# The gated DeltaNet rounds of a decoder kernel: the convolution's last tap from ScalarE, the two chunk inversions as one, and the state readout later in the round

## The chip, the cores and the metric

The kernel runs on one core of a Trainium2 chip. Its time is the device time of one execution in microseconds; the median of three is given. The core's engines run side by side and meet at semaphores: TensorE (PE in the profile) multiplies, VectorE (DVE), ScalarE (ACT) and GpSimd (POOL) work element by element, SyncE (SP) issues the weight transfers.

## The reference

One inference step of a trunk with two layers, for 256 prompt tokens in two chunks of 128 and for 8 sequences of 4 sampled tokens (288 columns in all). Layer 0 has the gated DeltaNet mixer, layer 1 a Mamba-2 mixer. Only the first is touched:

```python
proj = hn @ w_in                                  # q, k, v, z, a, b
qkv, new_buf = causal_conv(qkv, conv_buf, conv_w) # 4 taps, depthwise
qkv = silu(qkv)
q, k = l2norm(q) * 128**-0.5, l2norm(k)
beta, g = sigmoid(b), -exp(A_log) * softplus(a + dt_bias)
a_mat = (k*beta) @ k.T * decay * strict           # per chunk and head
t_mat = inverse(eye + a_mat)
u, w = t_mat @ (v*beta), t_mat @ (k*beta*exp(g))
# scan over chunks: v_new = u - w S;  o = (q*exp(g)) S + (q k.T * decay) v_new
# S = S*exp(g_last) + k_dec.T v_new.  Sampled tokens: the same rule on their own states
o = rmsnorm(o) * silu(z);  out = o @ w_out
```

All is float32. A product with weights is formed from three fp32r products: high x high, low x high, high x low part.

## The kernel before

**Projection.** Weights come as tiles of 2048 x 128 in two halves of 512 KB. SyncE loads a half into `ring`, ScalarE copies it to the high part `wh` (`upper`, L787; a tile's two halves are `ahead`), GpSimd subtracts to get the low part `wl` (`lower`, L324, four instructions for a half), and TensorE multiplies (`project`, L347 to L349) into one of two PSUM banks `psj`. A bank is reused when its consumer has counted up `took_act`.

**The DeltaNet rounds.** After six tiles ahead of the loop, a loop of 15 rounds and a last one outside it handle one pair of value heads each. In round m TensorE runs 48 *slots*, e = 0 to 47, of six projection matmuls for round m+1; that is six tiles: q and k (tiles T_GLOOP and +1), z of round m (+2, +3), v (+4, +5). Behind each slot `gdn_mix(m, e)` may insert matmuls of round m's attention. So the order on TensorE is written out by hand by slot number, and a wait in an insertion stops the projection too.

**What round m inserts.** e = 0: products of the chunks' keys and queries (counts `g_tok`). e = 3: transposes of `gMK` (L402, waits for `g_mk`), and 16 matmuls that read the sampled sequences' states, the *readout* (L407, waits for the state transfer `g_st_in`). e = 5: transposes of `gDE` (waits for `g_e1`). e = 7 to 19: the inversion of `eye + a_mat` in six levels, for each of the two chunks c apart: `inv_p(c, lv)` multiplies, VectorE masks (`mask_p`, L1448), `inv_q(c, lv)` multiplies, VectorE subtracts (`less_q`, L1459 and L1461). The chunks alternate, so that one has the array while the other is on VectorE. e = 10 waits for `g_bs`, an operation on VectorE (L1474) that stands behind tap 1 of v's convolution. e = 19: transposes of v. e = 21 to 31: values, states, outputs; e = 27 waits for `vnds` from ScalarE (L1000). e = 36: transposes of the normalized output (waits for `g_on`). e = 39: the column sums for the norms of the next q and k (L354).

**ScalarE in a round**, in this order: decay matrices (`g_dte`: six Relu, one Exp, L926 to L932), copies, take tiles q and k from `psj` (L855, L856), Silu of v, copies of values, z, Silu and squares of q and k, roots, take of tile +4, the transfers of the next round's rows, v parameters and states (`g_load`), take of tile +5. After a take comes `ahead`.

**VectorE in a round**: waits for the rows, copies the round's columns, forms `gMK` and `gMQ` (L1411), then the decayed products (L1417 to L1426, ending with `g_e1`), the sampled part (to L1434, `g_as`), then the six levels with the four taps of v's convolution among the first four (L1366 is tap 0, L1368 taps 1 to 3), and so on to the next q and k: taps, norms (`g_kn`).

Of the kernel before, what the change touches and what calls it, by code (L numbers as in the profile page):

```python
# [22 lines left out]
P = 128  # L23
D_MODEL = 2048
KT = D_MODEL // P
SEQ = 256
# [53 lines left out]
SMP_PE = {n: i + 1 for i, n in enumerate(("kmt", "smp", "ast", "sqs", "esp", "us", "osm"))}  # L80
SMP_ACT = {n: i + 1 for i, n in enumerate(("kmc", "asc", "qs", "vnds"))}
G_DVE_LINKS, S_DVE_LINKS = 19, 27
# [23 lines left out]
def packed(ap, lv):  # L106

    return ap.rearrange("p (j i s) -> p j i s", j=2, s=2 << lv)
# [25 lines left out]
def build(nc, weights, x_in, p_in, prm_in, cst_in, gpack, spack, gstate, sstate,  # L134
          y_out, gconv_out, sconv_out, gst_p, gst_s, sst_p, sst_s,
          g_rows, s_rows, h_spill, G_DVE, G_ACT, S_DVE, S_ACT):
    with ExitStack() as ctx:
# [24 lines left out]
        def carve(sizes):  # L162
            out, at = {}, 0
            for name, n in sizes:
# [13 lines left out]
                    ("pc", PC_G), ("co", 4 * CW), ("cc", 16), ("sc", 5 * GV), ("scc", 10), ("MS", 2 * NS),  # L178
# [16 lines left out]
        gcc = ga["cc"].rearrange("p (k c j) -> p k c j", k=4, c=NC)  # L195
        gscc = ga["scc"].rearrange("p (k j) -> p k j", k=5)
# [9 lines left out]
        gDE = ga["DE"].rearrange("p (c k j t) -> p c k j t", c=NC, k=2, j=2)  # L206
# [129 lines left out]
        def _(pe):  # L336
# [42 lines left out]
            def gdn_ready(m, e):  # L379
# [3 lines left out]
                if e == 10:  # L383
                    pe.wait_ge(S("g_bs"), m + 1)
                if e == 27:
                    pe.wait_ge(S("g_sample_act"), m * 4 + SMP_ACT["vnds"])

            def gdn_mix(m, e, more):
# [10 lines left out]
                if e == 3:  # L399
                    pe.wait_ge(S("g_mk"), m + 1)  # L400
                    for r in range(2):
                        mm = pe.transpose(psF[:, r * P:(r + 1) * P], gMK[:, 4 * r:4 * r + 4, :], ident)  # L402
                    mm.then_inc(S("g_sample_pe"), 1)
                    pe.wait_ge(S("g_st_in"), m * 16 + 16)
# [5 lines left out]
                if e == 5:  # L410
                    pe.wait_ge(S("g_e1"), m + 1)
                    for c in range(NC):
                        for j in range(2):
                            mm = pe.transpose(psB[:, (2 * c + j) * P:(2 * c + j + 1) * P], gDE[:, c, 1, j, :], ident)
# [6 lines left out]
                def inv_p(c, lv):  # L421
# [4 lines left out]
                    else:  # L426
                        pe.wait_ge(S(f"g_de{c}"), m * 6 + lv)
                    for j in range(2):
# [1506 lines left out]
```

## Time and profile before

| quantity | value |
|---|---|
| median of three runs | 2826.65 us (2825.04 to 2834.03) |
| the profiled execution | 2822.21 us, its span 2820.4 us |
| TensorE matmul busy | 2514.7 us, 89% |
| VectorE, ScalarE, GpSimd busy | 1486.1, 1170.1, 1666.4 us |
| mean granted TensorE clock | 0.950 of full speed |

The rounds of the DeltaNet layer lie between about 74 and 1340 us. The timeline view gives one row for a run of like instructions of one line: start, duration, engine, line, operation, output and input; in brackets how long the engine had been idle before it and what it waited for. A duration includes the pipeline's depth, so successive starts tell what an instruction occupies. "PEclk" is the granted clock of a stretch as a share of full speed (1.0 is 2.4 GHz, 0.5 is 1.2 GHz).

### The profile page before, as it was taken

To read this page: it belongs to the slowest core of one execution; us is meant where nothing else is said; L and a number is where in the kernel's file an instruction comes from. 1 tells how busy PE (TensorE), PEld (TensorE's weight loads), DVE (VectorE), ACT (ScalarE), POOL (GpSimd) and SP (SyncE) were. 2 spreads that over 40 slices of the span, in tenths; PEclk is the share of its full clock that TensorE was granted. 3 is DMA by queue.
4 is the path that set the end of the run, shared out by engine and by line. 5 is a ranking of instruction groups with operands and counts; after the bars stand their busy time and mean duration, and the time that the engine had idled before them with its cause. 6 is when DMAs were issued, how large, how long until landed. Compare 5 with 4: busy or idle time off the path is not lost.

```text
span 2820.4 us, 57876 instructions
## 1 busy us (share of the span) xinstructions
PE 2514.7 (89%) x20918; PEld 2295.1 (81%) x20918; DVE 1486.1 (53%) x3373; ACT 1170.1 (41%) x2073; POOL 1666.4 (59%) x2236
## 2 busy tenths in 40 slices
PE   6988898988988889898999988888898889799997
PEld 5877777877877778787999888877887779699987
DVE  5555555555556555555132426676767776722242
ACT  4433343433343344434333444444454435433343
POOL 4544444434444454434887667666766677598765
PEclk8999999999999999999999999999999999899999
DMA  4333333323333333322644336545654466354433
GB/s 183 115 128 120 135 120 135 107 105 109 129 120 128 127 135 120 127 95 103 215 154 153 115 124 237 180 134 174 228 189 147 162 214 201 108 213 150 153 119 116
DMA packets 126773, 410.86 MB, mean 146 GB/s; under 512 B 21344, under 2 KB 37984, under 8 KB 122112
## 3 DMA queue, kind: packets, MB, share of 16 engines
q1 hardware_dynamic: 81216, 295.75, 30.0%
q10 hardware_dynamic: 45504, 114.38, 11.7%
q8 instruction: 37, 0.61, 0.1%
q14 instruction: 16, 0.13, 0.0%
HBM read 363.47 MB, written 46.61 MB: 145 GB/s over the span
## 4 chain that ended last, share of the span: by engine, by line
issue 34%; POOL 31%; PE 22%; DVE 10%; ACT 2%; DMA 1%; POOLq 0%; ACTq 0%; DVEq 0%
POOL wl L324 31%; PE psj L347 6%; PE psj L349 6%; PE psj L348 6%; DVE arena L1368 5%; DVE arena L1366 2%; ACT arena L1205 1%; DVE arena L1706 1%; DVE arena L1697 1%; PE psA L736 1%; PE psE L354 1%; DVE arena L1704 1%; PE psE L691 0%; PE psA L354 0%; DMA arena<-s_rows_d 0%
## 5 line engine op out<-in xcount | busy, mean ns | idle before, releaser
L324 POOL TENSOR_TENSOR wl<-ring,wh 128x256 fp32r<-128x256 f32 x2232 | 1666.2, 785 | 1131.4 <-ACT wh L787 1130.3
L347 PE MATMUL psj<-xh,wh 128*128 128x288 f32 x4400 | 1390.5, 316 | 105.3 <-DVE arena L1474 59.6
L348 PE MATMUL psj<-xl,wh 128*128 128x288 f32 x4400 | 1316.2, 299 | 0.0
L349 PE MATMUL psj<-xh,wl 128*128 128x288 f32 x4400 | 1311.4, 298 | 0.0
L347 PEld LDWEIGHTS psj<-xh,wh 128*128 128x128 f32 x4400 | 841.4, 191 | 182.1 <-issue 80.9
L348 PEld LDWEIGHTS psj<-xl,wh 128*128 128x128 f32 x4400 | 845.2, 192 | 6.5 <-issue 3.9
L349 PEld LDWEIGHTS psj<-xh,wl 128*128 128x128 f32 x4400 | 845.3, 192 | 0.0
L787 ACT ACTIVATE wh<-ring 128x1024 fp32r<-128x1024 f32 x558 | 564.9, 1056 | 245.1 <-PE psj L349 217.3
L1368 DVE SCALAR_TENSOR_TENSOR arena<-arena 128x256 f32<-128x256 f32 (+1 forms) x672 | 287.9, 494 | 2.6
L855 ACT ACTIVATE arena<-psj 128x256 f32<-128x256 f32 x112 | 43.1, 385 | 472.6 <-PE psj L349 462.0
L407 PE MATMUL psD<-h 128*32 128x256 f32 x512 | 75.1, 460 | 32.8 <-DMA h<-gstate_d 32.8
L1621 DVE TENSOR_TENSOR arena<-Y,arena 128x288 f32<-128x288 f32 x32 | 14.7, 458 | 163.2 <-ACT arena L1076 162.5
L1597 DVE TENSOR_TENSOR h<-h,psj 128x288 f32 x32 | 14.5, 454 | 162.1 <-PE psj L349 162.1
L1366 DVE TENSOR_SCALAR arena<-arena 128x256 f32<-128x256 f32 x224 | 93.5, 486 | 0.0
L678 PE MATMUL psA<-cst,arena 128*128 128x128 f32 x16 | 7.2, 448 | 94.5 <-ACT arena L1205 94.5
L407 PEld LDWEIGHTS psD<-h 128*32 128x32 f32 x512 | 34.1, 130 | 70.0 <-DMA h<-gstate_d 36.7
L678 PEld LDWEIGHTS psA<-cst,arena 128*128 128x128 f32 x16 | 3.3, 206 | 96.4 <-ACT arena L1205 96.4
L1587 DVE COPY Y<-psj 128x288 f32 x22 | 10.1, 457 | 131.6 <-PE psj L349 131.6
L1459 DVE TENSOR_TENSOR arena<-arena,psF 128x128 f32<-128x128 f32 x80 | 23.1, 289 | 91.2 <-PE psF L359 91.2
L1076 ACT ACTIVATE arena<-psj 128x288 f32<-128x288 f32 x32 | 13.1, 410 | 130.5 <-PE psj L349 130.5
L1448 DVE TENSOR_TENSOR arena<-psC,cst 128x128 f32<-128x128 f32 x96 | 27.1, 282 | 70.7 <-PE psC L359 70.7
L359 PE MATMUL psA<-arena 128*64 128x64 f32 x1408 | 64.0, 236 | 0.0
(311 smaller groups left out, 2999.2 us busy)
## 6 DMA issues: line engine op xcount, KB each, us to landing
ring<-weights_d SPq DMA_DIRECT2D x558, 512.0 KB, 3.3
h<-gstate_d ACTq DMA_DIRECT2D x16, 1024.0 KB, 8.7
gst_s_d<-h ACTq DMA_DIRECT2D x16, 1024.0 KB, 3.9
h<-sstate_d ACTq DMA_DIRECT2D x32, 512.0 KB, 6.3
sst_s_d<-h ACTq DMA_DIRECT2D x32, 512.0 KB, 5.0
arena<-g_rows_d ACTq DMA_DIRECT2D x16, 864.0 KB, 4.6
arena<-s_rows_d ACTq DMA_DIRECT2D x8, 1152.0 KB, 7.6
h_spill_d<-h ACTq DMA_DIRECT2D x2, 2304.0 KB, 7.8
```

Source lines behind the costliest of these rows:

```text
L324: ins = pool.tensor_tensor(wl[:, s, n:n + 2], ring[:, s, n:n + 2], wh[:, s, n:n + 2].bitcast(F32), ALU.subtract)
L347: pe.matmul(out, w_h, xh[:, kt, :], start=(kt == 0), stop=False)
L348: pe.matmul(out, w_h, xl[:, kt, :], start=False, stop=False)
L349: mm = pe.matmul(out, w_l, xh[:, kt, :], start=False, stop=(kt == KT - 1))
L354: return pe.matmul(out, ones, rhs, start=start, stop=stop)
L359: mm = pe.matmul(bank[r:r + 64, cols], lhsT[:, r:r + 64], rhs, start=True, stop=True)
L407: mm = pe.matmul(psD[NS * n:NS * n + NS, 0:2 * P], (gMK, gMQ)[n][:, b, :], gS[:, b, :, :], start=(b == 0), stop=(b == DEC_B - 1))
L736: pe.matmul((psA, psB, psC, psF)[g][:, :], sBM[rows, r, :], sXT[rows, :], start=True, stop=True).then_inc(S("s_sp"), 1)
L787: act.activation(wh[:, hc % 4], ring[:, hc % 4], ACT.Copy).then_inc(wh_ready, 1)
L855: return lambda bank: (act.activation(U[:, i, UP:UC], bank[:, 0:SEQ], ACT.Copy), act.activation(U[:, i, US:UW], bank[:, SEQ:T], ACT.Copy))[1]
L1366: ins = dve.tensor_scalar(out, src, tap(i, j), None, ALU.mult)
L1368: ins = dve.scalar_tensor_tensor(out, src, tap(i, j), out, ALU.mult, ALU.add)
```

## The change

Five things are done together, all in the DeltaNet layer.

1. **Last tap.** When ScalarE takes a q, k or v tile, it first writes `gCR` = tile x tap 3 with one more Copy with a scale (`g_take_u`). VectorE adds three taps in place of four, and its tap 0 accumulates (`begun=True`).
2. **One inversion.** The two chunks are inverted together: `inv_p(lv)` at e = 7 + 2 lv, `inv_q(lv)` at e = 8 + 2 lv, each with both chunks' matmuls. VectorE's instructions span both chunks (128 x 256). `inv_q` counts `g_qd` after its first half and `g_qe` after its second.
3. **Readout.** `gMK`'s transposes and the readout go from e = 3 to e = 18, now into `psD`; `gMK` and `gMQ` are formed after `g_as`.
4. **Decays.** The decay matrices of round m+1 are formed at the end of round m, between the takes of tiles +4 and +5 (`g_decays`); the round's columns are copied by VectorE behind `states(0)`. Beta is multiplied in ahead of the wait for `g_tok`. The rows are loaded early in round m, once `g_rf` is counted; `EG` keeps the columns that are needed later.
5. **Slots.** The wait for `g_bs` goes from e = 10 to e = 12; v's transposes from 19 to 17; the insertions of 21 to 31 each one slot earlier; output transposes from 36 to 37; the column sums from 39 to 40.

```diff
-                if e == 10:
+                if e == 12:
                     pe.wait_ge(S("g_bs"), m + 1)
-                if e == 27:
+                if e == 26:
                     pe.wait_ge(S("g_sample_act"), m * 4 + SMP_ACT["vnds"])
...
+                def inv_p(lv):
+                    if lv == 0:
+                        pe.wait_ge(S("g_d"), m + 1)
+                        pe.wait_ge(S("g_sample_act"), m * 4 + SMP_ACT["asc"])
+                    else:
+                        pe.wait_ge(S("g_dd"), m * 5 + lv)
+                    for u in range(4):
+                        mm = halves(psC, slice(u * 64, (u + 1) * 64), gAT[:, u, :], half(gDE[:, 0], lv, 0)[:, u])
+                    mm.then_inc(S("g_p"), 1)
+                def inv_q(lv):
+                    pe.wait_ge(S("g_pm"), m * 6 + lv + 1)
+                    if lv < 5:
+                        for u in range(4):
+                            mm = halves(psA, slice(u * 64, (u + 1) * 64), gDE[:, 1, u, :], half(gP[:, :], lv, 0)[:, u])
+                        mm.then_inc(S("g_qd"), 1)
+                    for u in range(4):
+                        mm = halves(psE, slice(u * 64, (u + 1) * 64), gP[:, u, :], half(gDE[:, 1], lv, 1)[:, u])
+                    mm.then_inc(S("g_qe"), 1)
...
-                if e == 39 and more:
+                if e == 40 and more:
                     pe.wait_ge(S("g_su"), m * 4 + 2)
                     gdn_norm(m + 1)
...
+            def g_take_u(i, m, bank):
+                act.wait_ge(S(("g_pq_in", "g_pv_in")[i // 2]), m * 16 + 16)
+                act.activation(gCR[:, i, :], bank[:, 0:T], ACT.Copy, scale=gpc_tap[i // 2][:, i % 2, CONV_W - 1:CONV_W])
+                take_u(i, gU)(bank).then_inc(took_act, 1)
...
                 if full:
                     tile_wait(m, per, T_GLOOP + 4)
-                    take_u(2, gU)(psj[T_GLOOP % 2]).then_inc(took_act, 1)
+                    g_take_u(2, m + 1, psj[T_GLOOP % 2])
                     ahead(m, per, T_GLOOP + 6)
+                if full:
+                    g_decays(m + 1)
...
+                def less_q(lv):
                     if lv < 5:
+                        dve.wait_ge(S("g_qd"), m * 5 + lv + 1)
+                        D = half(gDE[:, 0], lv, 0)
+                        dve.tensor_tensor(D, D, packed(psA[:, 0:2 * P], lv), ALU.subtract).then_inc(S("g_dd"), 1)
+                    dve.wait_ge(S("g_qe"), m * 6 + lv + 1)
+                    E = half(gDE[:, 1], lv, 1)
+                    dve.scalar_tensor_tensor(E, packed(psE[:, 0:2 * P], lv), cst[:, K_BM, K_ROW + lv:K_ROW + lv + 1],
+                                             E, ALU.mult, ALU.add).then_inc(S("g_de"), 1)
```

ScalarE at a round's end, before: L787 is `ahead` of tile +6, L860 to L862 the three transfers, L855 the take of tile +5.

```order
L787 ACTIVATE wh<-ring 128x1024 [waits half_done]
L787 ACTIVATE wh<-ring 128x1024 [waits half_done,w_in1]
L860 ISA [waits g_sp_out,g_cv_out,g_st_out,g_y]
L860 DMA arena<-g_rows_d 128x1728
L861 ISA
L861 DMA arena<-gpack_d 128x56
L862 ISA
L862 DMA h<-gstate_d 128x2048
```

The same place in the change; L854 is the added Copy with the tap as scale.

```order
L779 ACTIVATE wh<-ring 128x1024 [waits half_done]
L779 ACTIVATE wh<-ring 128x1024 [waits half_done,w_in1]
L875 ACTIVATE arena<-arena 128x128 [waits g_r_in,g_dtx]
L875 ACTIVATE arena<-arena 128x128 x3
L878 ACTIVATE arena<-arena 128x32 x2
L131 REGISTER_ALU
L881 ACT_TABLE_LOAD
L881 ACTIVATE arena<-arena 128x576 [waits act_order]
L867 ISA [waits g_sp_out,g_cv_out,g_st_out,g_y]
L867 DMA h<-gstate_d 128x2048
L787 REGISTER_ALU
L854 ACTIVATE arena<-psj,arena 128x288 [waits g_pv_in,half_done]
```

The decays, with the load of Exp's table between them, now stand ahead of the take of tile +5.

VectorE at a round's start, before:

```order
L1404 COPY arena<-ccol 128x16
L131 ISA
L1407 ISA [waits dve_order]
L1407 COPY arena<-arena 128x10
L1409 REGISTER_ALU
L1411 TENSOR_TENSOR h<-arena,cst 128x256 [waits g_kn]
L1411 TENSOR_TENSOR h<-arena,cst 128x256
L1417 TENSOR_TENSOR arena<-arena,cst 128x512 [waits g_dte]
L131 REGISTER_ALU
L1418 TENSOR_TENSOR arena<-arena 32x64 [waits dve_order]
L1422 TENSOR_TENSOR arena<-arena,psC 128x512 [waits g_tok]
```

And in the change; the first row is the branch of the loop, which stands behind the wait for all six takes:

```order
L1597 UNCONDITIONAL_BRANCH [waits took_act]
L1597 ISA
L1434 COPY arena<-arena 128x2x8 [waits g_dte]
L1435 COPY arena<-arena 128x2
L1436 TENSOR_TENSOR arena<-arena,cst 128x512
L1437 TENSOR_TENSOR arena<-arena 32x64
L131 ISA
L1438 TENSOR_TENSOR arena<-arena 32x64 [waits dve_order]
L1439 TENSOR_TENSOR arena<-arena 128x512
L131 REGISTER_ALU
L1443 TENSOR_TENSOR arena<-arena,psC 128x512 [waits g_tok,dve_order]
```

The columns and `gMK` are gone from the start; one small and two 128 x 2 copies and two multiplications with both inputs in SBUF (L1438, L1439) stand ahead of the wait for `g_tok`.

VectorE in level 1 of the change (L1472 is `mask_p`, L1385 tap 1, L1496 counts `g_bs`, L1482 and L1485 are `less_q`):

```order
L1472 TENSOR_TENSOR arena<-psC,cst 128x64x4 [waits g_p]
L1385 SCALAR_TENSOR_TENSOR arena<-arena 128x256
L1385 SCALAR_TENSOR_TENSOR arena<-arena 128x32
L1385 SCALAR_TENSOR_TENSOR arena<-arena 128x256
L1385 SCALAR_TENSOR_TENSOR arena<-arena 128x32
L131 REGISTER_ALU
L1496 TENSOR_TENSOR arena<-cst,psD 32x64 [waits g_sample_pe,dve_order]
L1480 REGISTER_ALU
L1482 TENSOR_TENSOR arena<-arena,psA 128x64x4 [waits g_qd]
L1485 SCALAR_TENSOR_TENSOR arena<-psE,cst,arena 128x64x4 [waits g_qe]
```

The subtraction that the next `inv_p` waits for (`g_dd`) stands behind the tap.

## Rows read from the trace of the kernel before

**Rows 1.** Windows, the 15 rounds: stretch, length, busy by engine, PEclk, DMA share, GB/s

```profile
152.50:1340.20 1187.70, 1062.09 (x10345) 924.43 (x10344) 663.57 (x1860) 472.20 (x942) 532.28 (x724) 0.95 0.34 120
```

**Rows 2.** TensorE's waits, 152 to 1340 us: us in total, times, longest

```profile
PE psj L347 <- DVE arena L1474: 55.9, 15, 4.0
PE psD L407 <- DMA h<-gstate_d: 30.8, 15, 3.3
PE psE L536 <- DVE arena L1538: 23.8, 14, 1.7
PE psF L402 <- DVE h L1411: 10.9, 15, 1.0
```

**Rows 3.** Timeline of TensorE in one round: start, us, engine, line, operation

```profile
393.44 0.65 PE L354 MATMUL psB<-arena,cst 128*128 128x288 f32 x2
...
401.11 0.27 PE L394 MATMUL psA<-cst,arena 128*128 128x128 f32 x1
...
402.55 0.40 PE L347 MATMUL psj<-xh,wh 128*128 128x288 f32 x1
...
439.13 0.40 PE L347 MATMUL psj<-xh,wh 128*128 128x288 f32 x1
...
440.13 0.45 PE L359 MATMUL psE<-arena 128*64 128x64 f32 x8
440.41 0.63 PE L359 MATMUL psA<-arena 128*64 128x64 f32 x16
440.98 0.40 PE L347 MATMUL psj<-xh,wh 128*128 128x288 f32 x1
```

**Rows 4.** Timeline of ScalarE, end of a round and start of the next

```profile
395.65 2.01 ACT L787 ACTIVATE wh<-ring 128x1024 fp32r<-128x1024 f32 x2
...
400.51 0.39 ACT L855 ACTIVATE arena<-psj 128x256 f32<-128x256 f32 x1 [2.85 <-PE psj L349]
...
402.89 1.28 ACT L926 ACT_TABLE_LOAD   x1
404.63 1.28 ACT L926 ACTIVATE arena<-arena 128x128 f32<-128x128 f32 x4 [0.45 <-DVE arena L1407]
...
406.37 0.68 ACT L932 ACTIVATE arena<-arena 128x576 f32<-128x576 f32 x1
```

**Rows 5.** Timeline of GpSimd, same round

```profile
396.79 12.40 POOL L324 TENSOR_TENSOR wl<-ring,wh 128x256 fp32r<-128x256 f32 x16 [6.94 <-ACT wh L787]
420.00 6.00 POOL L324 TENSOR_TENSOR wl<-ring,wh 128x256 fp32r<-128x256 f32 x8 [10.81 <-ACT wh L787]
```

**Rows 6.** Timeline of VectorE, same round

```profile
407.08 0.84 DVE L1417 TENSOR_TENSOR arena<-arena,cst 128x512 f32<-128x512 f32 x1 [0.98 <-ACT arena L932]
...
410.67 0.69 DVE L1426 TENSOR_TENSOR arena<-cst,arena 128x512 f32<-128x512 f32 x1
...
412.71 0.21 DVE L1434 TENSOR_TENSOR arena<-cst,arena 32x64 f32<-32x64 f32 x1
...
423.23 2.82 DVE L1368 SCALAR_TENSOR_TENSOR arena<-arena 128x256 f32<-128x256 f32 x4
...
432.34 1.20 DVE L1368 SCALAR_TENSOR_TENSOR arena<-arena 128x256 f32<-128x256 f32 x4
```

**Rows 7.** Timeline of TensorE, behind slot 23

```profile
450.63 0.71 PE L492 MATMUL psA<-h 32*128 32x128 f32 x4
```

**Rows 8.** Timeline of ScalarE, the same stretch

```profile
454.37 0.62 ACT L1000 ACTIVATE h<-psA,arena 128x128 f32<-128x128 f32 x2
```

**Rows 9.** Timeline of TensorE: the readout in two rounds

```profile
408.93 5.33 PE L407 MATMUL psD<-h 128*32 128x256 f32 x32 [2.34 <-DMA h<-gstate_d]
...
801.09 3.65 PE L407 MATMUL psD<-h 128*32 128x256 f32 x32 [1.61 <-DMA h<-gstate_d]
```

**Rows 10.** Windows, two stretches of that round; PEclk is third from the end

```profile
408.90:414.20 5.30, 5.27 (x33) 2.38 (x33) 4.15 (x11) 0.00 (x0) 0.29 (x1) 0.68 0.55 196
...
427.10:430.50 3.40, 3.40 (x36) 2.94 (x35) 0.84 (x3) 0.00 (x0) 0.00 (x0) 0.51 0.42 154
```

More of the change, by code:

```diff
@@ L398, in gdn_mix @@
                         .then_inc(S("g_tok"), 1)
-                if e == 3:
+                if e == 5:
+                    pe.wait_ge(S("g_e1"), m + 1)
+                    for c in range(NC):
+                        for j in range(2):
+                            mm = pe.transpose(psB[:, (2 * c + j) * P:(2 * c + j + 1) * P], gDE[:, 1, 2 * c + j, :],
+                                              ident)
+                    mm.then_inc(S("g_dt"), 1)
+                if e == 6:
+                    for j in range(2):
+                        mm = pe.transpose(psE[0:NS, 64 + NS * j:64 + NS * (j + 1)], gATS[:, j, :], ident[0:NS, 0:NS])
+                    mm.then_inc(S("g_sample_pe"), 1)
@@ new lines, in gdn_mix @@
+                for lv in range(6):
+                    if e == 7 + 2 * lv:
+                        inv_p(lv)
+                    if e == 8 + 2 * lv:
+                        inv_q(lv)
+                if e == 7:
+                    for j in range(2):
+                        mm = pe.matmul(psD[0:NS, 256 + NS * j:256 + NS * (j + 1)], gATS[:, j, :], gAS[:, j, :],
+                                       start=True, stop=True)
+                    mm.then_inc(S("g_sample_pe"), 1)
+                if e == 12:
+                    for j in range(2):
+                        mm = pe.matmul(psD[0:NS, 320 + NS * j:320 + NS * (j + 1)], gBS[:, j, :], gNS[:, j, :],
+                                       start=True, stop=True)
+                    mm.then_inc(S("g_sample_pe"), 1)
@@ L421, in inv_p @@
-                def inv_p(c, lv):
-                    if lv == 0:
-                        pe.wait_ge(S("g_d"), m + 1)
-                        pe.wait_ge(S("g_sample_act"), m * 4 + SMP_ACT["asc"])
-                    else:
-                        pe.wait_ge(S(f"g_de{c}"), m * 6 + lv)
-                    for j in range(2):
-                        mm = halves((psC, psE)[c], slice(j * 64, (j + 1) * 64), gAT[:, 2 * c + j, :],
-                                    half(gDE[:, c, 0], lv, 0)[:, j])
-                    mm.then_inc(S(f"g_p{c}"), 1)
@@ L449, in gdn_mix @@
-                for lv in range(6):
-                    if e == 7 + 2 * lv:
-                        if lv > 0:
-                            inv_q(1, lv - 1)
-                        inv_p(0, lv)
-                    if e == 8 + 2 * lv:
-                        inv_p(1, lv)
-                        inv_q(0, lv)
-                if e == 7:
-                    for j in range(2):
-                        mm = pe.matmul(psD[0:NS, 256 + NS * j:256 + NS * (j + 1)], gATS[:, j, :], gAS[:, j, :],
-                                       start=True, stop=True)
-                    mm.then_inc(S("g_sample_pe"), 1)
@@ L885, in take @@
                 tile_wait(0, 0, k)
-                take_u(i, gU)(psj[k % 2]).then_inc(took_act, 1)
+                g_take_u(i, 0, psj[k % 2])
                 ahead(0, 0, k + 2)
@@ L1533, in gdn_body @@
                 states(0)
+                if full:
+                    columns(m + 1)
                 dve.wait_ge(S("g_rs2"), m + 1)
```

252 lines of the change are left out of this document (115 added, 137 removed).

## The prediction

> **What bounds the kernel now.** I read the page first: matmuls are busy 89% of the span, but its chain of waits ends in the dense stages, which the change does not touch. So the question is what one DeltaNet round costs, and how many there are. The windows view over 152.5 to 1340.2 us gives 15 rounds in 1187.7 us, 79.2 each [rows 1]; with the one ahead and a part of the last, about 15.5 rounds carry the change. GpSimd is busy 35.5 us of a round, VectorE 44.2, ScalarE 31.5: TensorE sets the pace, and it does so with four stalls that the view of waits names [rows 2]. Per round: 3.7 at e = 10 (`g_bs`, behind tap 1), 2.05 at e = 3 for the states, 0.73 at e = 3 for `gMK`, 1.7 at e = 36 for the normalized output. That is 8.1 us per round. What moves no stall and no clock moves nothing.
>
> The timeline of one round gives the small units. Call N the end of the column sums: N = 393.71 (last L354 at 393.44) [rows 3]. From N to the insertion of e = 0 at 401.11 there are nine slots, 0.82 each with their share of switching; the insertion lasts to 402.55, 1.44. Between insertions a slot takes 1.00 (439.13 to 440.13), so each place with an insertion costs about 0.2 beside its own matmuls. One chunk's `inv_p` occupies 0.28, one chunk's `inv_q` 0.57 [rows 3].
>
> **The start of a round.** Weights: GpSimd begins on the first half of e = 0's tile at 396.79, N + 3.1, and takes 12.40 / 4 = 3.1 for a half [rows 5]. In the change the take ahead of it is longer by one Copy; L855, the nearest row, takes 0.39, of which I count 0.33 as occupancy [rows 4]. The half is ready at N + 6.5. The column sums stand at e = 40, so only seven slots, not eight, lie between N and e = 0: TensorE comes at N + 5.7 and waits 0.8. Before it came after the half was ready.
>
> Decays: the second conversion ended at 397.66 (395.65 + 2.01), N + 3.95; with the Copy N + 4.3. Then Relu 1.74 (404.63 to 406.37), the table 1.28, Exp 0.68 [rows 4]: N + 8.0. The take of tile +5 follows, 0.33 + 0.47, and with it the `took_act` that VectorE's loop waits for: VectorE starts at N + 8.9. Without the move it started its masks at 407.08, N + 13.4 [rows 6]. From there to the end of L1426 at 411.36 it took 4.3. The change adds two small copies and one 32-partition multiply, together about 0.5. But it also starts while GpSimd works: before, GpSimd's sixteen instructions end at 409.19 [rows 5], so only the first two of these ran beside it; in the change its fourth half ends near N + 16.5, and six instructions with both inputs in SBUF run beside it. What that costs is in the taps: four of them take 2.82 beside GpSimd (423.23, GpSimd busy 420.0 to 426.0) and 1.20 alone (432.34) [rows 5, 6], 0.41 more each. Four more instructions under it: 1.6. So `g_e1` comes at N + 8.9 + 4.3 + 0.5 + 1.6 = N + 15.3. TensorE reaches e = 5 at N + 6.5 + 0.8 + 1.44 + 4.1 = N + 12.8: a stall of 2.5. Then `g_as`: before, 1.56 after `g_e1` (411.36 to 412.92) [rows 6], one instruction shorter now, of which TensorE fills about 0.4 with its transposes: 1.1. New stalls 0.8 + 2.5 + 1.1 = 4.4 against 2.8 removed: +1.6. The bounds of the middle term: 0.1 stall if no instruction is delayed, 4.3 if each of six waits for a whole one of GpSimd (12.40 / 16 = 0.78).
>
> The Trainium skill, page "SBUF — State Buffer", section "Who interferes with whom", says why: a VectorE instruction with two SBUF inputs and a GpSimd instruction that reads SBUF lock each other out for their whole length. The taps agree in kind; with 0.41 for each the sum stands as above, and with a whole GpSimd instruction for each it would be the second rival.
>
> **The levels.** `inv_p` now occupies 0.57, `inv_q` 1.13, a level 3.7 as before. What stalls is the subtraction behind the taps. Level 0: mask ends about 1.15 after `inv_p` begins, copies 0.5, four taps, of which two beside GpSimd (2.0), subtraction 0.4: 4.2 to 4.6; TensorE is back after 0.57 + 1.0 + 1.13 + 1.0 and some 0.2 for the small product behind e = 7 = 3.9. Stall 0.5. Level 1: 1.15 + 2.82 + 0.2 + 0.4 = 4.6 against 3.7: stall 0.9, down to none if GpSimd is through by then. Level 2, tap at 1.20, fits. `g_bs` is there by e = 12. So 3.7 becomes 1.4: -2.3 (bounds -3.7 and -1.4).
>
> **The rest of a round.** The last tap: 4 x 0.30 = 1.2 leaves VectorE twice a round, where it waits anyway but for level 3. Silu of v: the take is 0.33 longer and TensorE is two slots earlier, about +0.6 at e = 17 (0 to 1.0). Values: ScalarE takes z when slot 23 is done, at T = 450.63 [rows 7], and is through with L1000 at 454.99 [rows 8], T + 4.4. Before, TensorE was at e = 27 at just that time. Now the matmuls L492 (0.64) stand at e = 22 and the wait at e = 26, a slot and 0.64 sooner: +1.5, nearly fixed. At e = 37 the chain through ScalarE's Silu, squares and root from e = 31 is as long as before, and TensorE has one slot more behind e = 31 but no longer the state products, which are a little longer than a slot: +0.3. The readout at e = 18 finds its states landed long before. Two insertions fewer: -0.4.
>
> Sum without the clock: 1.6 - 2.3 + 0.6 + 1.5 + 0.3 - 0.4 = +1.3 us per round.
>
> **The clock.** The readout takes 5.33 in one round and 3.65 in another [rows 9], and in the first the granted clock is 0.68 of full; behind the stall of e = 10 it is 0.51, so 1.2 GHz [rows 10]. Both come after stalls: 0.7 + 2.3 at e = 3, 3.7 at e = 10. The stall of 1.7 at e = 36 is followed by none. Low readouts are 10 of 16, 1.7 each, 1.1 a round; the low stretch of level 1 costs about half of its 3.4 less what TensorE would have waited, 1.3. So 2.4 a round. In the change 2.5 + 1.1 at e = 5 and 6 are much like the old e = 3, and a low stretch there is likely, partly under level 0's stall: 1.1. Behind the levels' short stalls I expect none, behind 1.5 and 2.0 (e = 26, 37) one in some rounds: 0.4. So 1.5 in place of 2.4: -0.9.
>
> Net +0.4 a round, x 15.5 = +6 us: 2822.2 becomes about 2828 for a profiled execution. The median of the runs lies 4.4 above the profiled one, so 2833.
>
> **Rivals.** First, *the clock stays up* (faster): if the stalls of e = 5 and 6 are short enough, because GpSimd's work falls elsewhere, all 2.4 come back, and the middle term is nearer its lower bound: 1.3 - 2.4 - 0.4 = -1.5 a round, -23, 2804. For it: the largest stall, 3.7, is gone. Against: VectorE now starts inside GpSimd's busy stretch in every round, the two being tied to the same conversions. Second, *the lock costs a whole GpSimd instruction* (slower): 0.37 more on each of six instructions, 2.2 on e = 5 (4.3 at most, less what overlaps the clock), with the low stretch kept: about +1.9 a round on top of the forecast, +29, 2862; halfway, +1 a round, 2849. It decides at e = 5: a stall above 3.3 there. L1417, 0.84 against 0.69 for its like alone [rows 6], speaks for less; the tap's row shows 0.41, half of it. Third, *old and new stalls trade places exactly* and the slots are bound by ScalarE's chain anyway: 2826, inside the forecast's own range.
>
> **Numbers.** Forecast and third case 0.40, own range 2822 to 2840. First rival, with milder forms of it, 0.22. Second, with milder forms, 0.38. Less than 0.3%, 8.5 us, a measurement of this kernel can't tell from none: faster is below 2818, slower above 2835. The forecast's case falls inside in three quarters, else above: faster 0.24, same 0.34, slower 0.42. The range runs from the first rival's 2804 to the second's 2862.
>
> **What would show it.** In the profile after: TensorE's wait for L1474's successor gone, and in its place waits at L1445's product (e = 5) of 2 to 3 us, at e = 6 of 1, at e = 0 of 0.8 for `wl`, at e = 26 of 1.5 for ScalarE's L1015; e = 37 at 2.0. The six instructions from L1436 on at 0.4 more than alone. One low stretch of clock a round, not two, and the readout at 3.65. Wrong would be: no wait at e = 5 (then faster), or one above 3.3, or two low stretches (then slower), or a wait for states at e = 18.

## The result

The changed kernel takes 2853.8 us (median of six runs, 2840.6 to 2857.8) against 2822.8 for the kernel before: ratio 1.0103, 95% interval 1.0075 to 1.0131. It is slower, by 1%. A second set of six runs on another occasion gave 2843.5 us, ratio 1.0086 (1.0062 to 1.0110). The forecast was 2833 in a range of 2804 to 2862, with "slower" its likeliest side: the side and the range hold. The reason given for the size does not: the stalls came out shorter than forecast, and the clock, which was to give something back, took the most.

The profiled execution took 2840.6 us with a span of 2838.8 (granted clock 0.943). It is the fastest of its six, so it shows the loss too small; the second profiled execution of the same kernel took 2843.3 us (span 2841.5) at 0.942. Within the first six the time goes with the clock: 2840.6 and 2842.4 us at 0.943, 2852.6 at 0.941, 2855.0, 2855.3 and 2857.8 at 0.938.

The windows view over 15 rounds of the changed kernel, from one write of `Y` to the one 15 rounds later (columns: length; busy time and instructions of PE, PEld, DVE, ACT, POOL; PEclk, DMA share, GB/s), and its view of TensorE's waits over 152 to 1370 us (total, times, longest):

```profile
158.20:1355.70 1197.50, 1077.32 (x10345) 940.73 (x10344) 625.25 (x1518) 494.14 (x1000) 547.14 (x727) 0.94 0.34 119
```

```profile
PE psE L528 <- DVE arena L1560: 30.4, 15, 2.0
PE psB L404 <- DVE arena L1445: 27.2, 15, 1.8
PE psj L348 <- DVE arena L1452: 20.3, 15, 1.4
PE psj L348 <- ACT h L1015: 13.6, 14, 1.0
PE psj L348 <- POOL wl L325: 13.3, 16, 1.0
PE psF L464 <- ACT arena L972: 7.6, 14, 0.5
PE psC L360 <- DVE arena L1482: 6.3, 16, 1.6
PE psC L495 <- ACT arena L1007: 2.8, 14, 0.2
```

Fifteen rounds take 1197.5 us where they took 1187.7 [rows 1]: 0.65 us more for each. Of the other 8.6 us of difference between the spans, 5.1 lie ahead of the first write of `Y` and 3.6 behind the last. The eight waits add up to 121.5 us, 8.1 per round; those of before, with a small fifth one, to 8.3 [rows 2]. So the stalls only changed places: there is none at `g_bs` or at the states any more, and in their stead there are five new ones of 0.5 to 1.8 us, at `e = 5`, 6, 26, 0 and 17, and one of 0.4 in the levels. The one ahead of the output transposes grew from 1.7 to 2.0. VectorE is busy 38 us less, ScalarE 22 more, over the 15 rounds. What is left for the 0.65 is TensorE working more slowly: it is busy 15 us more.

The timeline of TensorE behind two of those stalls, in the round whose `e = 0` is at 402.5 us (start, duration; in brackets the idle time before and what ended it):

```profile
402.52 0.40 PE L348 MATMUL psj<-xh,wh 128*128 128x288 f32 x1 [0.81 <-POOL wl L325]
...
410.93 0.66 PE L404 MATMUL psB<-cst,arena 128*128 128x128 f32 x4 [1.83 <-DVE arena L1445]
412.96 0.40 PE L348 MATMUL psj<-xh,wh 128*128 128x288 f32 x1 [1.38 <-DVE arena L1452]
...
413.74 0.29 PE L350 MATMUL psj<-xh,wl 128*128 128x288 f32 x1
...
414.80 0.44 PE L348 MATMUL psj<-xh,wh 128*128 128x288 f32 x1
...
415.66 1.12 PE L360 MATMUL psC<-arena 128*64 128x64 f32 x16
...
418.37 0.69 PE L360 MATMUL psA<-arena 128*64 128x64 f32 x16
```

The windows view of the two places (the second begins with the output transposes of `e = 37`; last columns PEclk, DMA share, GB/s):

```profile
411.00:419.45 8.45, 7.08 (x76) 0.80 0.59 212
468.98:475.50 6.52, 6.50 (x26) 0.50 0.32 108
```

One projection matmul goes from 0.29 to 0.44 us some 3 us behind the stall at `e = 5`, one `inv_p` takes 1.12 us instead of 0.69. Behind `e = 37` the clock is at 0.50 of full, so 1.2 GHz, for 6.5 us. The trace's record of the clock lets one count the low stretches of each round; a long one is counted as two or three pieces. In 14 rounds there are 30 before the change: 10 behind the stalls at `e = 3`, 17 behind `e = 10`, 3 behind the output transposes. After it there are 40: 27 behind `e = 5` and 6, up to three in a row, and 13 behind `e = 37`, in seven of the rounds (27 and 18, in ten rounds, in the second profile). Counted from one write of `Y` to the next, the rounds that begin with the low clock of `e = 37` and have it in the front too take 80.2 to 81.7 us in the two profiles, the others 77.7 to 79.2.

VectorE and GpSimd at the same time, for the step on `g_e1`:

```profile
404.99 0.28 DVE L1434 COPY arena<-arena 128x16 f32<-128x16 f32 x1 [3.10 <-ACT arena L849]
...
405.85 0.75 DVE L1437 TENSOR_TENSOR arena<-arena 32x64 f32<-32x64 f32 x1
...
407.23 0.67 DVE L1439 TENSOR_TENSOR arena<-arena 128x512 f32<-128x512 f32 x1
...
408.66 1.09 DVE L1444 TENSOR_TENSOR arena<-arena,cst 128x512 f32<-128x512 f32 x1
409.78 1.09 DVE L1445 TENSOR_TENSOR arena<-cst,arena 128x512 f32<-128x512 f32 x1
...
417.55 2.69 DVE L1385 SCALAR_TENSOR_TENSOR arena<-arena 128x256 f32<-128x256 f32 x4
...
421.93 2.35 DVE L1385 SCALAR_TENSOR_TENSOR arena<-arena 128x256 f32<-128x256 f32 x4
...
425.98 1.20 DVE L1385 SCALAR_TENSOR_TENSOR arena<-arena 128x256 f32<-128x256 f32 x4
```

```profile
399.30 5.93 POOL L325 TENSOR_TENSOR wl<-ring,wh 128x256 fp32r<-128x256 f32 x8 [7.41 <-ACT wh L779]
405.51 7.32 POOL L325 TENSOR_TENSOR wl<-ring,wh 128x256 fp32r<-128x256 f32 x8 [0.28 <-ACT wh L779]
```

Beside GpSimd the mask and the subtraction behind it (L1444, L1445) take 1.09 us instead of the 0.69 of [rows 6], 0.40 more each, and a 32-partition product 0.75 instead of about 0.2. That is the size that was taken, not a whole GpSimd instruction. But not every one of the six is longer: L1439 takes 0.67, though GpSimd works beside it, in all rounds, and L1436 begins in the short pause between GpSimd's two rows. Why L1439 is spared is open.

### The profile page after: what moved, and what is told of

It reads as the page before. It is cut to its first block, busy times and chain, and to the rows that moved or that the text cites. A ratio compares the mean times of both kernels' runs of the same rounds, so it can differ in the third digit from the quotient of the medians.

```text
span 2838.8 us, 57663 instructions
## 1 busy us (share of the span) xinstructions
PE 2534.7 (89%) x20918; PEld 2315.3 (82%) x20918; DVE 1450.1 (51%) x3005; ACT 1192.9 (42%) x2136; POOL 1678.8 (59%) x2236
## 4 chain that ended last, share of the span: by engine, by line
POOL 43%; issue 40%; PE 11%; DVE 5%; ACT 1%; POOLq 1%; DMA 0%; ACTq 0%; DVEq 0%; SPq 0%
POOL wl L325 43%; PE psj L348 3%; PE psj L350 3%; PE psj L349 3%; DVE arena L1385 2%; DVE arena L1383 1%; ACT arena L1222 0%; PE psE L355 0%; POOLq L329 0%; PE psA L728 0%; DMA ring<-weights_d 0%; POOLq L323 0%; DVE h L1797 0%; PE psA L355 0%; PE psE L683 0%
## 5 line engine op out<-in xcount | busy, mean ns | idle before, releaser
L349 PEld LDWEIGHTS psj<-xl,wh 128*128 128x128 f32 x4400 | 855.3, 194 | 6.4 <-issue 3.9
L1385 DVE SCALAR_TENSOR_TENSOR arena<-arena 128x256 f32<-128x256 f32 (+1 forms) x672 | 299.0, 511 | 2.0
L854 ACT ACTIVATE arena<-psj,arena 128x288 f32<-128x288 f32 x64 | 31.8, 496 | 249.1 <-PE psj L350 242.4
L1472 DVE TENSOR_TENSOR arena<-psC,cst 128x256 f32<-128x256 f32 x96 | 40.8, 425 | 133.8 <-PE psC L360 133.8
L360 PEld LDWEIGHTS psC<-arena 128*64 128x64 f32 x1536 | 58.7, 151 | 25.3 <-issue 14.2
L360 PE MATMUL psC<-arena 128*64 128x64 f32 x1536 | 72.8, 243 | 6.5 <-DVE arena L1482 6.3
L1485 DVE SCALAR_TENSOR_TENSOR arena<-psE,cst,arena 128x256 f32<-128x256 f32 x96 | 46.1, 481 | 39.4 <-PE psE L360 37.1
```

The costliest lines, as they stand in the source:

```text
L349: pe.matmul(out, w_h, xl[:, kt, :], start=False, stop=False)
L360: mm = pe.matmul(bank[r:r + 64, cols], lhsT[:, r:r + 64], rhs, start=True, stop=True)
L854: act.activation(gCR[:, i, :], bank[:, 0:T], ACT.Copy, scale=gpc_tap[i // 2][:, i % 2, CONV_W - 1:CONV_W])
L1385: ins = dve.scalar_tensor_tensor(out, src, tap(i, j), out, ALU.mult, ALU.add)
L1472: dve.tensor_tensor(half(gP[:, :], lv, 0), packed(psC[:, 0:2 * P], lv), half(bc(cst[:, K_LEV + lv, :], 1, 4), lv, 0), ALU.mult) \
L1485: dve.scalar_tensor_tensor(E, packed(psE[:, 0:2 * P], lv), cst[:, K_BM, K_ROW + lv:K_ROW + lv + 1], E, ALU.mult, ALU.add).then_inc(S("g_de ...
```

## The experiments

All times are medians; ratios are against the kernel before, run beside it on the same chip. "Low" is the count of low-clock pieces in 14 rounds of the profiled execution, front (up to `e = 7`, the first level included) / levels and middle / output transposes, "round" the mean length of these 14 rounds, "waits" the sum of TensorE's waits per round. These three columns come from one profiled execution of each kernel, which is not the median: it is the slowest of its set for "`e = 5` overfilled" (2814.4 us) and for "values and front a slot later" (2764.2), the fastest for the changed kernel. Filling is idle work laid into a stall; the experiments below explain the rows.

| kernel | us | ratio (95%) | round | waits | low |
|---|---|---|---|---|---|
| before | 2822 | 1 | 78.95 | 8.3 | 10/17/3 |
| changed | 2853.8 | 1.0103 (1.0075, 1.0131) | 79.67 | 8.1 | 27/0/13 |
| changed, again | 2843.5 | 1.0086 (1.0062, 1.0110) | 80.35 | 8.0 | 27/0/18 |
| tap back on VectorE | 2837.7 | 1.0059 (1.0040, 1.0078) | 79.72 | 7.6 | 32/3/12 |
| both stalls overfilled | 2815.5 | 0.9969 (0.9951, 0.9987) | 78.29 | 4.0 | 0/12/0 |
| `e = 5` overfilled | 2804.4 | 0.9936 (0.9911, 0.9961) | 78.26 | 6.0 | 0/6/13 |
| both stalls filled to fit | 2804.8 | 0.9937 (0.9919, 0.9955) | 77.73 | 5.2 | 18/0/0 |
| before, overfilled | 2825.0 | 1.0014 (0.9997, 1.0032) | 79.04 | 1.9 | 0/0/3 |
| before, filled to fit | 2795.0 | 0.9907 (0.9886, 0.9929) | 77.15 | 3.1 | 2/0/6 |
| outputs at `e = 38` | 2818.8 | 0.9987 (0.9969, 1.0005) | 78.52 | 7.7 | 14/0/14 |
| and values a slot later | 2768.4 | 0.9811 (0.9778, 0.9845) | 75.06 | 5.2 | 29/0/0 |
| and filled to fit | 2729.5 | 0.9676 (0.9655, 0.9697) | 72.66 | 2.9 | 0 |
| values and front a slot later | 2750.0 | 0.9744 (0.9712, 0.9776) | 74.52 | 4.6 | 19/9/0 |
| and filled to fit | 2712.6 | 0.9610 (0.9588, 0.9632) | 71.42 | 2.4 | 0 |

One sum, an estimate from these columns, holds for all rows. Take from a round its waits and its filling (0.109 us for each idle transpose, from start to start). What is left is 67.0 to 67.3 us in the three kernels with no or hardly a low piece, 70.7 in the kernel before, and 71.6 and 72.4 in the changed one. Over the whole table it grows by roughly 1.4 to 2.4 us for each low piece that a round has. So in the profiles the changed round is longer by 0.7 and 1.4 us because low clock takes 0.9 and 1.7 more, while the waits give back 0.2 and 0.3.

The theory: the stalls before and after are equal, and the loss is the low clock that TensorE works at behind the new ones. The rivals: the scaled copies on ScalarE delay what TensorE waits for; or the clock is a symptom that costs nothing.

### The last tap back on VectorE

```diff
-G_DVE_LINKS, S_DVE_LINKS = 15, 27
+G_DVE_LINKS, S_DVE_LINKS = 17, 27
...
-                act.activation(gCR[:, i, :], bank[:, 0:T], ACT.Copy, scale=gpc_tap[i // 2][:, i % 2, CONV_W - 1:CONV_W])
...
-                for j in range(PRE):
+                for j in range(CONV_W):
...
-                    if lv < PRE:
+                    if lv < CONV_W:
```

> The kernel after the change with its last convolution tap back on VectorE: five links of a DeltaNet convolution there again, and no scaled copy out of the projection's bank on ScalarE. All else, the new places of the insertions and the four-block levels, stays. Theory (the 1.0% come from the new places of the insertions and the clock behind them): the tap is worth little by itself, 2850 +- 10 us; the wait at e = 5 grows by about 0.3, level 3 gets a stall of 0.5 to 1, e = 0 loses its 0.9 for the weights. Rival (the scaled copies on ScalarE delay the conversions of weights and the decays, and this is what the change pays for): 2825 +- 8 us, as before the change.

2837.7 us: some 6 to 16 us faster than the changed kernel in its two sets, between the two expectations and nearer the theory's. Its waits, against those of the changed kernel above: the weights at `e = 0` 6.0 instead of 13.3, the values' transposes at `e = 17` 2.2 instead of 7.6, and `e = 5` 32.1 instead of 27.2. The levels cost 9.7 instead of 6.3. In all 0.5 a round, 7 us. So ScalarE's copies can have cost part of the loss, with the weights' conversion queued behind them, but the larger part stays when they are gone. How large their part is remains open: the interval overlaps with that of the changed kernel's second set, and the round of the profile is no shorter (79.72 against 79.67 and 80.35).

### Idle work in the stalls

```diff
                 if e == 5:
+                    for k in range(24):
+                        pe.transpose(psF[:, (k % 4) * P:(k % 4 + 1) * P], ident, ident)
                     pe.wait_ge(S("g_e1"), m + 1)
...
                 if e == 37:
+                    pe.wait_ge(S("g_s2"), m + 1)
+                    for k in range(28):
+                        pe.transpose(psE[:, (k % 4) * P:(k % 4 + 1) * P], ident, ident)
                     pe.wait_ge(S("g_on"), m + 1)
```

> The kernel after the change with 24 idle 128x128 transposes of the identity ahead of TensorE's wait at e = 5 and 28 ahead of its wait at e = 37, into banks that nothing uses there: about 1.3 and 1.5 us of TensorE work (estimated from 0.055 us for one 128-column operation at full clock), laid into stalls of 1.8 and 2.0 us. They compute nothing that is used. Theory (the time went into the low clock that follows these two stalls): the stalls as such stay, but TensorE is busy in them, so the low stretches behind them disappear: fewer than 20 such stretches in 14 rounds instead of 40, mean clock above 0.96, time 2800 to 2830 us. Rival (the low clock does not come from these stalls, or costs nothing because other waits absorb it): 2850 to 2865 us, clock 0.94.

2815.5 us: TensorE is given 5.8 us of useless work a round, more than the two stalls are long, and the kernel is 28 to 38 us faster. Low pieces fall from 40 or 45 to 12, the granted clock of the whole span rises to 0.962. The rival that calls the clock a symptom falls. The 12 that are left lie at a new place, behind the waits of 0.9 at `e = 26` and 0.2 after it, which no low clock had followed before.

With the filling at `e = 5` alone:

```diff
                 if e == 5:
+                    for k in range(24):
+                        pe.transpose(psF[:, (k % 4) * P:(k % 4 + 1) * P], ident, ident)
```

> The kernel after the change with the 24 idle transposes ahead of the wait at e = 5 alone; the stall of 2.0 us at e = 37 is left as it is. Theory (each of the two stalls calls low clock of its own; in the profiled execution of the changed kernel 26 or so of the 40 low stretches lie at 18 to 22 us behind the write of Y, behind e = 5 and 6, and 14 at 76 to 80, behind e = 37): those behind e = 5 go, those behind e = 37 stay or become more, 14 to 20 stretches in 14 rounds, 2825 to 2838 us. Rival (one stall is enough to lower the clock somewhere in the round, so filling one of them gains nothing): 28 or more stretches, 2848 to 2858 us.

2804.4 us, better than both expectations, with 19 low pieces. The 27 pieces behind `e = 5` are gone, those behind `e = 37` stay (13), and six come elsewhere. The stall at `e = 5` is thus the dearer one. The second filling made the kernel 11 us slower: its 28 transposes take 3.1 us in a stall of 2.0, so it runs over by 1.1 a round. What it is worth at the right length no run shows by itself.

The same done to the kernel before, 10 and 28 transposes at `e = 3` and 52 at `e = 10`:

```diff
                 if e == 10:
+                    for k in range(52):
+                        pe.transpose(psB[:, (k % 4) * P:(k % 4 + 1) * P], ident, ident)
                     pe.wait_ge(S("g_bs"), m + 1)
```

> The kernel before the change, with idle transposes laid into its stalls: 10 ahead of gMK and 28 ahead of the states at e = 3 (about 0.55 and 1.5 us), 52 ahead of g_bs at e = 10 (about 2.9 us). Theory (the low clock of the kernel before is worth 2.4 us a round, as the prediction put it): about 30 low stretches become fewer than 5, 15.5 x 2.4 = 37 us less, 2786 us. Rival (the low stretch behind e = 10 lies where VectorE binds the levels anyway, so only the readout's 1.1 a round come back): 2805 us. Second rival (nothing comes back): 2822 us.

2825.0 us, as slow as without, though hardly a low piece is left. It looks like the second rival, but the timeline of TensorE at `e = 10` says otherwise:

```profile
422.57 0.40 PE L359 MATMUL psC<-arena 128*64 128x64 f32 x8
422.90 5.90 PE L385 MATMUL psB<-cst 128*128 128x128 f32 x52
```

One transpose takes 0.11 us, not 0.055, so 52 of them cover the stall of 3.7 us [rows 2] and 1.9 more, and those at `e = 3` run over by 1.4. Lengths that fit settle it (at `e = 3` 5 and 16 in place of 10 and 28):

```diff
-                    for k in range(52):
+                    for k in range(30):
                         pe.transpose(psB[:, (k % 4) * P:(k % 4 + 1) * P], ident, ident)
                     pe.wait_ge(S("g_bs"), m + 1)
```

> The kernel before the change with idle transposes that fit its stalls. In the run with 10, 28 and 52 of them one took 0.112 us, twice the estimate, so that they reached beyond the stalls: 52 took 5.65 us in a stall of 3.7. Now 5 ahead of gMK, 16 ahead of the states, 30 ahead of g_bs: 0.56, 1.8 and 3.4 us. Theory (the low clock costs 2.4 us a round before the change; the longer fillings ran over by about 2.6 a round and hid that): at most 6 low stretches in 14 rounds, 2822 - 15.5 x 2.4 = 2785 us. Rival (that low clock costs nothing, since the level behind e = 10 waits for VectorE anyway): 2822 +- 4 us.

And in the changed kernel, against the run with 24 and 28:

```diff
-                    for k in range(24):
+                    for k in range(12):
...
-                    for k in range(28):
+                    for k in range(14):
```

> The changed kernel with idle transposes that fit: 12 ahead of the wait at e = 5 (1.35 of 1.8 us), 14 ahead of that at e = 37 (1.57 of 2.0 us). Theory (the low clock behind these two costs 3.2 us a round, not the 1.5 of the prediction): under 14 low stretches in 14 rounds, 2848 - 15.5 x 3.2 = 2798 us. Rival (a stall of 0.4 us that is left still lowers the clock): 30 stretches or more, 2840 us.

The kernel before gains 27 us (0.9907), 1.7 a round; the changed kernel 44 us (0.9937 from about 1.0095), 2.8 a round, with 8 and 18 low pieces left (those of the changed kernel all in the front, behind the 0.5 us left of the stall at `e = 5` and the unfilled 1.4 at `e = 6`). Both are a little less than the theory's 2.4 and 3.2. The mean round of the filled kernel before, 77.15, holds one of 83.7 us, its first, in which the rows came late and TensorE waited 4.2 us for `gMK`; the other 13 take 76.6, 2.3 less than without filling. The waits of the filled kernel before show that the stalls are covered and not moved:

```profile
PE psE L542 <- DVE arena L1544: 23.8, 14, 1.7
PE psD L413 <- DMA h<-gstate_d: 7.3, 11, 1.2
PE psF L406 <- DVE h L1417: 6.7, 7, 4.2
PE psj L347 <- DVE arena L1480: 4.9, 15, 0.6
```

So low clock is worth at least 1.7 us a round before the change and at least 2.8 after it. With the stalls filled in both, the changed kernel is 10 us slower, without filling 24 to 29: more than half of the loss is clock. Even the 10 us are not all stalls, since 18 low pieces stand against 8. The rounds that no low piece touches take 76.2 us in the filled changed kernel and 75.6 to 76.3, 75.9 in the mean, in the filled kernel before: 0.3 apart.

### The output transposes one slot later

```diff
-                if e == 37:
+                if e == 38:
                     pe.wait_ge(S("g_on"), m + 1)
```

> The kernel after the change with the transposes of the normalized output one slot later, at e = 38 instead of 37. Theory: the stall there falls from 2.0 to about 1.0 us a round, and with a stall that short the low stretch that follows it in four to six of the rounds is gone: 15.5 x 1.0 + 5 x 1.4 = 22 us less, 2830 us. Rival (TensorE is ahead of GpSimd's weights anyway and gives the slot back at e = 0): the wait for the weights there grows from 0.9 to 1.9 and the time stays 2850 us within 5.

2818.8 us: the kernel is level with the one before again (0.9987, interval to 1.0005). One number in one line gives back 25 to 35 us. The wait at this place fell from 2.0 to 1.25 and did not come back at `e = 0` (13.4 against 13.3), so the rival is out. But one part of the theory failed: a low piece behind the transposes is still there, and now in every round, where before it came in pairs in seven rounds; a stall of 1.25 us does not protect from it. What fell by half are the pieces of the front, 27 to 14, though nothing was moved there.

### The values one slot later too

```diff
-                if e == 26:
+                if e == 27:
                     pe.wait_ge(S("g_sample_act"), m * 4 + SMP_ACT["vnds"])
...
-                if e == 30:
+                if e == 31:
                     pe.wait_ge(S("g_sample_act"), m * 4 + SMP_ACT["kmc"])
```

(The insertions of 22 to 29 move by one in the same way.)

> As the run with the output transposes at e = 38, and in addition the six insertions of the new values, states and outputs (e = 22 to 30) each one slot later, the wait for ScalarE's new values at e = 27 instead of 26. Theory: the stall of 1.2 us at e = 26 goes, TensorE puts a slot of the projection into it; the work behind it starts when it did, so the stall at e = 38 is 2.0 again; against the run with e = 38 alone about 1.0 us a round less, 2815 us, if the low stretch behind e = 38 does not come back; with it 2825. Rival (weights of GpSimd bound the round): all of it reappears at e = 0, 2850 us.

2768.4 us, 47 less than the theory gave. The wait of 1.1 at `e = 26` went as expected, but the one at `e = 38` did not return: it is gone altogether. The timeline of ScalarE in the changed kernel, and below it in this one, shows why:

```profile
459.78 0.60 ACT L1024 ACTIVATE arena<-psF 128x512 f32<-128x512 f32 x1
462.21 0.41 ACT L939 ACTIVATE arena<-psj 128x288 f32<-128x288 f32 x1 [1.83 <-PE psj L350]
...
467.26 0.30 ACT L1031 ACTIVATE arena<-arena,small 128x6 f32<-128x6 f32 x1
```

```profile
443.27 0.60 ACT L1024 ACTIVATE arena<-psF 128x512 f32<-128x512 f32 x1
443.76 0.41 ACT L939 ACTIVATE arena<-psj 128x288 f32<-128x288 f32 x1
...
448.81 0.30 ACT L1031 ACTIVATE arena<-arena,small 128x6 f32<-128x6 f32 x1
```

Between the squares of the output (L1024) and their root (L1031) ScalarE takes the second half of z from a projection's bank (L939), a conversion and the next q and k. In the changed kernel it waits 1.83 us there, for TensorE: the bank is complete only with the slot behind the insertion of `e = 30`. The stall at `e = 37` was TensorE waiting for a chain that had waited for TensorE. With the insertion one slot later the bank comes ahead of it, L1031 ends 5.8 us behind the start of L1024 instead of 7.8, and the stall is gone.

The kernel before has the same insertion at `e = 31`, and its ScalarE does not wait there in any round:

```profile
461.47 0.60 ACT L1009 ACTIVATE arena<-psF 128x512 f32<-128x512 f32 x1
461.96 0.41 ACT L918 ACTIVATE arena<-psj 128x288 f32<-128x288 f32 x1
...
467.01 0.30 ACT L1016 ACTIVATE arena<-arena,small 128x6 f32<-128x6 f32 x1
```

So the change itself made this wait, by moving the insertion from 31 to 30 (its fifth point), and the run puts it back. It also moves the wait of `e = 26`; what each of the two moves is worth alone was not run.

### Front insertions one slot later, and both filled

```diff
-                if e == 5:
+                if e == 6:
                     pe.wait_ge(S("g_e1"), m + 1)
...
-                if e == 40 and more:
+                if e == 39 and more:
                     pe.wait_ge(S("g_su"), m * 4 + 2)
```

> As the run with the values and the output transposes one slot later (2768 us), and in addition: all insertions of e = 5 to 20 one slot later, the column sums of the next round at e = 39 instead of 40, and in the last round the lowering of the next stage's x by VectorE behind level 3 instead of 4. Theory (TensorE fills a stall with a slot wherever the chain behind it starts later than the slot): the stall of 1.8 at e = 5 becomes 0.8 and the one of 0.9 at e = 0 goes, the low clock behind them becomes less: 1.9 a round and 0.5 to 1 of clock, 2768 - 15.5 x 2.5 = 2729 us. Rival (VectorE's chain of the round, some 75 us from the column sums to the state update, binds by now): the wait moves to the column sums or to the levels and the time stays at 2765 +- 5 us.

2750.0 us, half of what the theory gave. The wait at `e = 6` is 1.05 instead of 1.8, but the one for VectorE's subtraction in the levels rose from 9.4 to 21.9 us in all, and nine low pieces lie behind it. The rival is right for the levels: TensorE waits for VectorE there, 1.5 us a round. That the taps beside GpSimd are what makes VectorE late was not tested.

With idle transposes that fit, on the version with the values a slot later and on this one (where they stand at `e = 6` and 7, 8 and 10 of them):

```diff
                 if e == 6:
+                    for k in range(10):
+                        pe.transpose(psF[:, (k % 4) * P:(k % 4 + 1) * P], ident, ident)
                     pe.wait_ge(S("g_as"), m + 1)
...
                 if e == 5:
+                    for k in range(14):
+                        pe.transpose(psF[:, (k % 4) * P:(k % 4 + 1) * P], ident, ident)
                     pe.wait_ge(S("g_e1"), m + 1)
```

> The kernel with values and output transposes one slot later (2768 us), with 14 idle transposes ahead of the wait at e = 5 (1.57 of 1.8 us) and 10 ahead of the wait for g_as at e = 6 (1.1 of 1.3 us). Theory: its 29 low stretches, all at 17 to 20 us behind the write of Y, go; the slots from 396 to 401 us take 1.00 again instead of 1.74 and 1.5: 2768 - 15.5 x 1.5 = 2745 us. Rival (what the clock gives back is waited for again at level 0 and 1, behind VectorE's taps): 2765 us.

> The kernel with the front insertions one slot later as well (2750 us), with 8 idle transposes ahead of the wait at e = 6 (0.9 of 1.05 us) and 10 ahead of g_as at e = 7 (1.1 of 1.4 us). Theory: the low stretches at 18 and 19 us go, those at 29, behind the stalls of the levels, may stay; 2735 us. Rival (TensorE only waits longer at the levels for VectorE, 1.5 a round there already): 2750 +- 5 us.

2729.5 and 2712.6 us, 39 and 37 less, more than expected both times. The windows view over 14 rounds of the second, and its waits:

```profile
150.60:1150.50 999.90, 969.92 (x9887) 1.00 0.39 133
```

```profile
PE psC L360 <- DVE arena L1486: 17.7, 31, 1.6
PE psj L348 <- POOL wl L325: 10.8, 17, 2.1
PE psj L348 <- DVE arena L1456: 4.4, 15, 0.3
```

TensorE is busy 970 of 1000 us, the filling counted in (2.0 us a round), and its granted clock is 1.00 through all 14 rounds, against 0.94 in the changed kernel; a round is 71.4 us, and no low piece is left, not even behind the levels' stalls, which are still there. This version beats the kernel before by 3.9% (3.7 to 4.1).

### The changed kernel again

> The changed kernel itself, unaltered, timed beside the next three on one chip. Theory and rival alike: 2850 +- 6 us, 1.010 of the kernel before. It tells how much of the 38 us between it and the kernel with idle transposes is the chip.

2843.5 us, ratio 1.0086, 10 us below the first set's median. The two intervals overlap, so the loss lies between some 17 and 37 us.

## Why the prediction was right, and where not

**What bounds the kernel.** Right: TensorE's stalls and its clock account for every run of the table, and VectorE's 38 us of work less do not show in it.

**The start of a round.** The wait for the weights at `e = 0` was 0.8 forecast and is 0.9. For `g_e1` the forecast was column sums + 15.3 us; it came at + 15.1 (395.75 to 410.87), with the masks at the size taken from [rows 6]. The stall at `e = 5` is 1.8, not 2.5, mostly because TensorE comes 0.5 later than thought, at + 13.35 (409.10): the weights of `e = 0` came 0.3 later (402.52, + 6.8), and the six slots and the insertion behind them took 0.2 more. At `e = 6` 1.4, forecast 1.1. In all 4.1 instead of 4.4. The rival with a whole GpSimd instruction for each is refuted by the 1.09 of L1444. Its price was also added up wrong: 2.2 on top of 2.5 make a stall of 4.7, not 4.3.

**The levels.** 1.4 forecast, 0.4 measured. Here the low clock itself was overlooked: the slots and `inv_p` that follow `e = 6` run at half clock, so TensorE comes to level 1 when VectorE is almost done. Once the front is filled, the same place costs 0.7, and once it is early too, as in the last kernel, 1.2. The forecast of 0.5 for level 0 doesn't follow from its own terms, which add up to 4.05, not 4.2 to 4.6.

**The rest of the round.** `e = 17`: 0.6 forecast, 0.5 measured. `e = 26`: 1.5 against 0.9. `e = 37`: 2.0, as forecast, but by luck. The chain from ScalarE's squares of the output to the transposes was taken to be "as long as before"; it is 9.2 us against 7.3, because of the 1.83 that ScalarE waits for TensorE's bank. And TensorE's own way from the output products to that place is 1.6 us longer than before (458.93 to 466.97, against 460.62 to 467.06), where +0.3 of stall had been worked out from one slot more less the state products. The two errors leave the +0.3; without the bank's wait some 0.2 of the stall would be left. The readout takes 3.65 us in every round, as said. The states are never waited for.

All stalls together: 9.9 forecast, 8.1 measured. The step "Sum without the clock: +1.3" comes out as +0.6 in the pair of filled kernels (10 us / 15.5), and as +0.3 in their rounds without a low piece.

**The clock.** This is the step that failed: "So 1.5 in place of 2.4: -0.9". The 2.4 before was fair: at least 1.7 by the filled run's time, 2.3 by the rounds of its profile. The 1.5 after should have been 2.8 or more. Two things in it were wrong. The low stretch behind `e = 5` and 6 was priced as one piece, 1.1 us, since the old one behind `e = 3` cost that, and it is two pieces on average (27 in 14 rounds, against 10). And at `e = 37` the old stall of 1.7, followed by low clock in 3 rounds of 14, was taken as a licence for one of 2.0; in 7 to 10 rounds of 14 the low clock comes, for 6.5 us in the round shown. With the measured +0.6 in place of +1.3, the wrong clock term would have made the sum -0.3 a round, a faster kernel. Errors of +0.7 and -2.0 a round cancel in part; what is left, 1.3 x 15.5 = 20 us, is the distance from 2833 to 2853.8. That the number came as near as that, and on the right side, is luck.

**The rival "the clock stays up"** did not happen, but the filled kernel shows what it would have been worth: 2804.8 us, against its 2804. The agreement to 1 us is chance, since 18 low pieces are left there and the idle work is not free.

**The last tap**, costed as 0.33 us of delay on each take, is worth -6 to -16 us when undone, the smaller number within the noise of the second set; the 0.5 a round of waits explain 7.

**Open.** What makes the clock fall behind one stall and not behind another is not settled by the length of that stall: 1.7 at the old `e = 36` was harmless in 11 rounds of 14 (in 8 once the front was filled), 1.25 at `e = 38` in none, and the 1.2 in the levels of the last kernel in all. The pieces also repeat in patterns over several rounds (78.3, 77.7, 79.2, 78.5 and then four of 81.5 us in both profiles, beginning at other rounds), so two executions of one kernel hold different numbers of long rounds. That this makes the 10 to 17 us between executions is not shown: the two profiled ones differ by 10 us over 14 rounds and by 2.6 in all.

## What to carry to other kernels

Where one in-order engine runs both the dense work and the insertions of a dependent chain, add up its stalls before and after, but also read at what clock it works behind each: here equal stalls with a worse clock cost 1%. Before pricing a stall, ask what the engine it waits for had itself waited for; a stall that hangs on the waiting engine's own earlier slot goes away by moving an insertion by one. Moving the output transposes by one slot and then the values by one was worth nearly 3% of this program's time (1.0095 to 0.9811). Put cheap idle work of the right length ahead of the stalls that remain: it must not run over: in the kernel before, fillings some 3.3 us a round too long ate all that the clock returned.

## What was not expected of the hardware

- An idle transpose of the 128x128 identity takes 0.11 us of TensorE at full clock (52 in 5.9 us), and a train of them keeps the granted clock at 1.00 through stalls that otherwise bring 0.50.
- Filling the stalls pays in its own right: 27 us in the kernel before, 44 in the changed one, 39 and 37 in the two improved ones.
- A stall can leave up to 6.5 us at half clock behind it (468.98 to 475.50 us), longer than three times the stall.
- A 32-partition product of VectorE took 0.75 us beside GpSimd (L1437) where its like takes 0.21 alone [rows 6]: the delay beside GpSimd was 0.4 to 0.5 us for small and large instructions alike, where there was one. L1439, 128 x 512 with two inputs in SBUF, had none (0.67).
